# Five SBUF tensors of a matmul stream at other offsets modulo 256 bytes

## What is computed

```python
h  = modulate(rmsnorm(x, norm1_w), shift1, scale1)          # 2048 tokens
hc = modulate(rmsnorm(ctx, norm1_w), ...)                    # 256 context tokens
conf_u, q, k, v, af, ab, r, sc_u = split(h @ w_in)           # one projection, 2848 columns
y = concat([conformer_conv(...), gla_output(...), short_conv(...)]) @ w_out
x = x + gate1 * y
h = modulate(rmsnorm(x, norm2_w), shift2, scale2)
gate, idx = top_k(softmax(h @ router_w).T, 256)              # 16 experts, 256 tokens each
hid = silu(h[idx] @ w1[e]) * (h[idx] @ w3[e])                # per expert, 1024 x 1024 each
x = x + gate2 * scatter_add(gate * (hid @ w2[e]))
out = rmsnorm(x, final_norm_w)
```

## Time and profile before

| | |
|---|---|
| median of 3 runs | 2157.4 us (2153.78 to 2158.72) |
| the profiled execution: time | 2155.37 us |
| its span | 2153.7 us |
| instructions in it | 35092 |
| PE busy | 2074.7 us, 96% |
| PE's share of the chain that ended last | 80% |

### The profile page before, as it was taken

How to read it: one execution, slowest core, us unless ns; L and a number is a source line. 1 busy time by engine, 2 the same in 40 slices (tenths; PEclk the granted TensorE clock), 3 DMA queues, 4 the chain that set the end, 5 groups by cost and what they waited for, 6 DMA issues and landing times.

```text
span 2153.7 us, 35092 instructions
## 1 busy us (share of the span) xinstructions
PE 2074.7 (96%) x13569; PEld 1815.5 (84%) x13569; DVE 1369.9 (64%) x2082; ACT 996.1 (46%) x1631; POOL 277.8 (13%) x357
## 2 busy tenths in 40 slices
PE   6999999999999899997999999999999999999996
PEld 4778888888878677785899999999999999999985
DVE  3664648995994577757555656556555665656557
ACT  5923454444531445431444544445444444445455
POOL 0001000100001010020011122111221112111120
PEclk9999999999999999998999999999999999999998
DMA  7463333333427665456357666576565765657565
GB/s 258 150 248 132 109 106 99 115 118 88 125 77 237 236 208 176 145 214 257 118 204 246 215 215 211 187 264 214 193 216 195 273 198 186 217 218 253 198 233 225
DMA packets 188285, 407.95 MB, mean 189 GB/s; under 512 B 15956, under 2 KB 53396, under 8 KB 187300
## 3 DMA queue, kind: packets, MB, share of 16 engines
q1 hardware_dynamic: 162212, 318.36, 42.6%
q0 software_dynamic: 25984, 88.39, 12.6%
HBM read 329.59 MB, written 77.12 MB: 189 GB/s over the span
## 4 chain that ended last, share of the span: by engine, by line
PE 80%; DVE 10%; ACT 3%; DMA 3%; issue 2%; SPq 1%; POOL 0%; DVEq 0%; ACTq 0%; POOLq 0%
PE bh L55 11%; PE bh L57 11%; PE bh L56 11%; PE bank L55 8%; PE bank L57 8%; PE bank L56 8%; PE eby L55 5%; PE eby L57 5%; PE eby L56 5%; DVE acc L854 3%; PE ebt L2283 1%; PE bank L1031 1%; DVE over L2012 1%; PE bank L1413 1%; DVE raw L2472 1%
## 5 line engine op out<-in xcount | busy, mean ns | idle before, releaser
L55 PE MATMUL bh<-xt_hi,shi 128*128 128x256 f32 x2048 | 572.2, 279 | 3.2 <-DVE slo L2436 2.7
L56 PE MATMUL bh<-xt_lo,shi 128*128 128x256 f32 x2048 | 571.6, 279 | 0.0
L57 PE MATMUL bh<-xt_hi,slo 128*128 128x256 f32 x2048 | 571.4, 279 | 0.0
L2436 DVE TENSOR_TENSOR slo<-raw,shi 128x1024 fp32r<-128x1024 f32 x384 | 456.0, 1221 | 156.9 <-ACT shi L2345 152.4
L2345 ACT ACTIVATE shi<-raw 128x1024 fp32r<-128x1024 f32 x384 | 389.8, 1052 | 127.1 <-PE eby L57 125.5
L55 PEld LDWEIGHTS bh<-xt_hi,shi 128*128 128x128 f32 x2048 | 385.3, 188 | 4.6 <-issue 2.5
L56 PEld LDWEIGHTS bh<-xt_lo,shi 128*128 128x128 f32 x2048 | 385.4, 188 | 0.6
L57 PEld LDWEIGHTS bh<-xt_hi,slo 128*128 128x128 f32 x2048 | 385.3, 188 | 0.0
L55 PE MATMUL bank<-h_hi,whi 128*128 128x512 f32 x704 | 283.4, 403 | 0.0
L57 PE MATMUL bank<-h_hi,wlo 128*128 128x512 f32 x704 | 275.4, 391 | 0.0
L56 PE MATMUL bank<-h_lo,whi 128*128 128x512 f32 x704 | 275.4, 391 | 0.0
(11 more groups left out here) (348 smaller groups left out, 3127.6 us busy)
## 6 DMA issues: line engine op xcount, KB each, us to landing
raw<-in_exp_w_dram SPq DMA_DIRECT2D x96, 2048.0 KB, 11.0
uT<-stage POOLq DMA_DIRECT2D x72, 256.0 KB, 2.7
xb<-in_ada_w_dram SPq DMA_DIRECT2D x24, 512.0 KB, 5.6
wraw<-in_w_in_dram SPq DMA_DIRECT2D x22, 512.0 KB, 5.4
adaw<-in_ada_w_dram SPq DMA_DIRECT2D x8, 1024.0 KB, 9.7
xb<-in_x_dram SPq DMA_DIRECT2D x16, 512.0 KB, 4.2
xt<-in_x_dram POOLq DMA_DIRECT2D x16, 512.0 KB, 5.3
x2d<-xt POOLq DMA_DIRECT2D x16, 512.0 KB, 3.0
```

What stands on the lines that cost most here:

```text
L55: nc.tensor.matmul(out, w_hi, x_hi, start=start, stop=False)
L56: nc.tensor.matmul(out, w_hi, x_lo, start=False, stop=False)
L57: return nc.tensor.matmul(out, w_lo, x_hi, start=False, stop=stop)
L2436: nc.vector.tensor_tensor(item_dst(slo, n), item_src(n), item_dst(shi, n), ALU.subtract).then_inc(S["w_lo_ready"], 1)
```

## The change

No instruction is added, taken away or moved on any engine; one wait is added on ACT. What changes is where tensors stand in SBUF. Modulo 256 bytes:

| product | stationary: before, after | moving: before, after | columns |
|---|---|---|---|
| projection, latents | `whi`, `wlo`: 0, 0 | `h_hi`, `h_lo`: 0, 192 | 512 |
| projection, context | `whi`, `wlo`: 0, 0 | `hc_hi`, `hc_lo`: 0, 192 | 256 |
| output projection | `ct`: 0, 192 | `wo`: 0, 192 | 512 |
| experts, gate and up | `shi[i]`, `slo[i]`: 0, 32 i | `xt`: 32, 192 | 256 |
| experts, down | `ht`: 0, 96 | `shi[i]`, `slo[i]`: 0, 32 i | 512 |

A gap of 192 bytes (`h_gap`) ahead of `h_hi` moves everything behind it, also what is allocated relative to `low` and `high`: the six `raw` buffers, the buffers `xb` and `adaw` that the first loads fill, the states and the tail's tensors all go from 0 to 192. `gap` grows by 64 bytes, so that `whi`, `wlo` and the stages stay at 0. `xs`, into which the tokens of an expert are gathered, goes from 0 to 96. `wraw`, the raw weights of the projection, goes from 224 to 160 (the first tile's too; the third tile's, `wraw2`, from 0 to 192).

To make room, `msq` of `phase_project` lies in `tok`, which is written later, and four small tensors of `phase_experts` become slices of one. `shi[3]` now lies over `found`, which before lay under `slo[2]`; so ACT waits for `list_ready` before it writes item 3 of the first expert. DVE waits for the same semaphore before its first item, before and after.

```diff
-        gap = sb("gap", [P, 8])
+        gap = sb("gap", [P, 24])
...
-        ssq, msq, rst = (sb(n, [P, 18]) for n in ("ssq", "msq", "rst"))
+        ssq, rst = (sb(n, [P, 18]) for n in ("ssq", "rst"))
+        msq = v.tok[:, :, :].rearrange("p e s -> p (e s)")[:, 0:18]
...
+        v.found_free = (S["list_ready"], 1)
...
-        shi = [sb(f"shi{i}", [P, D], F32R) for i in range(NR)]
-        slo = [sb(f"slo{i}", [P, D], F32R) for i in range(NR)]
+
+        def behind(shift):
+            at[0] += (shift - at[0]) % 256
+
+        shi, slo = [], []
+        for i, shift in enumerate((0, 32, 64, 96)):
+            behind(shift)
+            shi.append(sb(f"shi{i}", [P, D], F32R))
+            slo.append(sb(f"slo{i}", [P, D], F32R))
         xs_words = [sb(f"xs{i}", [P, D], F32R) for i in range(2)]
         xs = [t[:, :].bitcast(F32) for t in xs_words]
-        at[0] += 32
+        behind(192)
         xt_hi, xt_lo = sb("xt_hi", [P, KD, CAP], F32R), sb("xt_lo", [P, KD, CAP], F32R)
-        at[0] += 224
+        behind(96)
         ht_hi, ht_lo = sb("ht_hi", [P, FD, CAP], F32R), sb("ht_lo", [P, FD, CAP], F32R)
...
-        ssq, msq, rst, nt = (sb("f_" + n, [P, NT + 2]) for n in ("ssq", "msq", "rst", "nt"))
+        small = sb("f_small", [P, 4 * (NT + 2)])
+        ssq, msq, rst, nt = (small[:, i * (NT + 2):(i + 1) * (NT + 2)] for i in range(4))
...
                 for n in range(NR):
+                    if n == NR - 1:
+                        act.wait_ge(*v.found_free)
                     split(0, n)
...
+                hsb("h_gap", [P, 48])
+                low = nc.sbuf_base
                 v.h_hi, v.h_lo = hsb("h_hi", [P, L // NB, KD, NB], F32R), hsb("h_lo", [P, L // NB, KD, NB], F32R)
```

## The result

The changed kernel takes 2180.4 us (median of 4 runs, 2177.92 to 2181.76) against 2156.1 us (2153.78 to 2158.72) for the kernel before: a ratio of 1.0111, with a 95% interval of 1.0094 to 1.0129. It is slower by 24.3 us, where 11.6 us less had been forecast. The profiled execution took 2177.92 us, with a span of 2176.2.

A forecast was written before the change was run, and what follows sets the result against it. PE's matmul streams were taken as the bound. Savings of 7.0 + 0.8 + 0 + 0 + 3.8 = 11.6 us from the median 2157.4 gave 2146 us, the forecast's own range being 2140 to 2151.

The forecast's parts named there:

- If only equal offsets cost, each saves 3.3 ns: PE's matmul streams: only operands at equal offsets pay extra, 13.2 against 9.9 ns besides columns, so unequal ones save 3.3 ns.
- Latent projection: Projection's 2112 matmuls of 512 columns, distance 0 to 192: each saves 3.3 ns, 7.0 us in all.
- Context projection: Projection's some 150 matmuls of 256 columns, same step: 0.5 us saved, plus 0.3 us for the narrow first tile.
- Output projection: Both operands, ct and wo, go from 0 to 192 and stay equal to each other: nothing.
- Gate and up: Experts' 6144 matmuls, distance 32 to 192, 160, 128 or 96: nothing; bounds 61 us saved, 20 us lost.
- Down product: Experts' 1536 matmuls: three quarters, 1152, become unequal and gain 3.3 ns each, 3.8 us; the fourth buffer stays equal.
- The wait on ACT: ACT's added wait before item 3 of the first expert: nothing, with over 3 us of cover.
- The DMAs: Loads now written off a multiple of 256: nothing taken, upper bound 3 us lost in the first 40 us.
- The rest: Gathered tokens xs, msq in tok and four slices of one tensor, outside PE's streams: nothing.
- the first, that a larger distance would be faster still: Rival: cost falls with distance, so gate and up gain at least 20.3 us more, 2125.5 us; chance 0.2.
- The second, no effect: Rival: offsets do nothing, the 3.3 ns belongs to the stage, time stays at 2157 us; chance 0.2.
- The third, that gate and up lose what they had: Rival: all 6144 gate and up matmuls return to 120.0 ns, 20.3 us lost, 2166 to 2178 us; chance 0.19.

The follow-up runs named there:

- e4_other_half: Kernel before with the split weight buffers at 0, 32, 64, 96, tokens at 64 and hidden values at 224 bytes; 2171.74 us, ratio 1.0077.
- e1_h_back: Changed kernel with the projection, first loads and tail back on a multiple of 256 bytes, experts as changed; 2170.8 us, ratio 1.0068.
- e7_w_beside_h: Changed kernel with the projection's split weights also at 192, beside h, so their distance is 0; 2173.24 us, ratio 1.0078.
- e5_same_distances: Changed kernel with all tensors of the experts' products 64 bytes further on, so every distance stays; 2178.33 us, ratio 1.0103.
- e9_kick_turn: e3_far_gate_up plus one unused float32 transposition on PE ahead of each expert's first item; 2138.09 us, ratio 0.9917 to the kernel before.
- e3_far_gate_up: Kernel before with the tokens xt at 192 bytes in place of 32, all split weight buffers at 0; 2160.03 us, ratio 1.0015.
- e6_far_256_higher: e3_far_gate_up with h and all behind it 256 bytes further on, places modulo 256 kept; 2160.9 us, ratio 1.0024 to the kernel before.
- e10_kick_r: e9_kick_turn with a float32r transposition in place of the float32 one; 2139.9 us, ratio 0.9923 to the kernel before.
- e12_even_128: Kernel before with the tokens xt at 128 bytes, so gate and up have that distance in all buffers; 2173.12 us in one run.
- e13_kick_alone: Kernel before with only a float32 transposition ahead of each expert's gate and up, tokens still at 32; 2161.27 us, ratio 1.0026.

## Why the prediction was wrong

All prices that were measured, in ns for one matmul:

| distance, bytes | 256 columns | 512 columns |
|---|---|---|
| 0 | 119.3 to 120.0 | 226.7 to 228.4 |
| 32 | 116.7 or 117.8 (118.0 in `e4_other_half`) | 233.2 |
| 64 | 117.8 | 229.4 |
| 96 | 119.8 to 120.0 | 233.9 |
| 128 | 118.4 to 118.7, or 119.9 | 233.2 |
| 160 | 120.1 to 120.2 | 233.8 to 234.2 |
| 192 | 113.3 to 114.1, or 117.8; context 116.6 | 232.7 (down), 233.3 (latents) |
| 224 | 118.2 to 118.3 | 232.6 to 233.0 |

**The step that failed** is the reading drawn from the two streams of 256 columns and then used everywhere: "If only equal offsets cost, each saves 3.3 ns". For 512 columns equal offsets are the cheapest, and every other distance costs 2 to 7 ns more. The prediction had two products with 512 columns in its own rows, both at 0, and nothing to compare them with; it took over the price of the other form. It also gave all unequal distances one price, for which it had no reason from a row, since the kernel before had only the distance of 32 in such a stream.

1. *Latent projection*, forecast -7.0 us: the distance of 192 cost 6.5 ns more for each in a steady stretch, and 5.3 over the stage, instead of 3.3 less; 11 us in the stream and 8.3 in the stage. This is the reading's first failure, and `e1_h_back` and `e7_w_beside_h` undo it in two different ways.
2. *Context projection*, -0.5 us: right, from 119.5 to 116.6 ns; the forecast's signal was 116.7. It was the one place where the reading was applied to the form that it was read from, at equal against unequal. The 0.3 us for the narrow first tile had no ground: its slices lie 128 bytes apart, not 512, so that its distances are 0 and 128 by turns, before and after.
3. *Output projection*, nothing: right. Both operands moved to 192 and a matmul took 227.4 ns for 228.1.
4. *Gate and up*, nothing: failed. Unequal distances aren't one price, and one distance isn't either: at 32 bytes the first expert of the kernel before ran at 117.8 ns and the others at 116.7, which the prediction's rows, taken from one expert, did not show. Of the four, 192 gained 2.8 ns in the changed kernel, 128 lost 1.7, 160 and 96 lost 3.0 to 3.4; 8 us in all. The prediction had named this group as the place where it could fail.
5. *Down product*, -3.8 us: failed with the first. Three buffers lost 5 to 7 ns each, 7 us in all, and the fourth kept its 227. The prediction did ask the right question ("if the fourth is no different, it is not equality that costs"): the fourth is different, and it is the cheap one.
6. *The wait on ACT*, nothing: right, the way from the routing to the first expert went from 11.5 to 11.7 us.
7. *The DMAs*, nothing with 3 us as the bound: the bound came true. The first latent matmul is 2.7 us late; it comes at 64.5 to 66.2 us in the five kernels with the loads at 192, and at 62.2 to 63.6 in the eleven others. The mis-sized term rested on `wraw` over the whole span, against `xb`. The program writes `wraw` in pieces of 512 bytes and `xb` in pieces of 4096, so the two differ by more than their offset, and what the offset alone does to a landing can't be read from them; in the first 45 us the rows had the tenth. The rule of the Trainium skill that was weighed there ("DMA: Bandwidth & Descriptors", section "How a descriptor splits into AXI transactions") has the sign right and not the size: the estimate worked out from it gave 19% more beats, and the rate fell by a tenth.
8. *The rest*, nothing: right as far as the stages show.

The rivals: the first, that a larger distance would be faster still, is wrong for this kernel and holds a part of the truth, since 113.4 ns exist at 192. The second, no effect, is refuted by `e1_h_back` and `e7_w_beside_h`. The Trainium skill's page "TensorE: Matmul & The Clock Gate" (section "Step-by-step: what each phase is for") gives the two operands a read port each, and by it the load of the next stationary operand costs the running matmul nothing. The traces do not agree that its place is free: the same 256 columns took 113.9 to 120.2 ns by buffer in the changed kernel and in `e5_same_distances`. Whether the ports are what meets is not shown. The third, that gate and up lose what they had, came about in part: two of the four buffers went to 120 ns and a third to 118.4. It gave 2166 to 2178 us; what it left out is that the projection and the down product lose too.

**What is shown and what is open.** Shown: moving both operands together changes nothing, and moving one changes the price (`e5_same_distances`, `e7_w_beside_h`), in another way for 256 than for 512 columns. That it is the distance modulo 256 rests on less: on the 160 and 416 bytes of the down product, and on the latents and the output projection, whose distances by the program's addresses are 256 and 0 modulo 512 and whose matmuls take 227.9 and 228.1 ns. At one distance a stream can hold to more than one pace for hundreds of matmuls. What precedes it picks one at 192 bytes (the transposition, by `e9_kick_turn` against `e3_far_gate_up`; a stall, one way in `e6_far_256_higher` and the other in `e9_kick_turn`). At 32 bytes both paces stand in the kernel before, and the transposition exchanges them. Open: why. Two readers of the same memory that meet or miss each other would fit, and no run looks at them apart. It is also open why the transposition picks the better pace at 192 and, in fifteen experts, the worse one at 32; why the first expert differs from the rest in the kernel before, `e10_kick_r`, `e12_even_128` and `e13_kick_alone`; and whether the executions without a trace keep the same paces.

**The best version** is `e9_kick_turn`: 0.83% under the kernel before and 1.9% under the changed one. It needs both of its parts, as `e3_far_gate_up` (the distance alone, +0.15%) and `e13_kick_alone` (the transposition alone, +0.26%) show.

## What to carry to other kernels

Before offsets are moved, read what one matmul costs from start to start for each form by itself, and in more than one turn of the loop, since a price read at 256 columns had the wrong sign at 512 and a price read in one expert was not that of another; then change one distance in one stream, and read that stream again. Keep large loads at the start on the offset at which they run now, or price them by the rate in the stretch where nothing hides them. Where a steady stream costs more than it does elsewhere at the same distance, try what stands ahead of it too, and trust only the whole kernel's time.

## What the runs showed of the hardware that was not expected

- With the granted clock at 1.00, the matmuls of one stream take 113.4 to 120.2 ns (256 columns) or 226.7 to 234.3 ns (512 columns) by where their two operands stand to each other modulo 256 bytes and by the pace that the stream has fallen into. The spreads are 6.8 and 7.6 ns.
- A stream keeps its pace: 117.8 ns for 383 matmuls in `e3_far_gate_up`, 113.3 for 359 in `e9_kick_turn`, at the same addresses in the experts' stage. One transposition of 0.1 us ahead of an expert makes the difference, 384 x 4.4 ns = 1.7 us. The kernel before does it by itself: 117.8 ns in its first expert, 116.7 in the others.
- Loads from DRAM into SBUF ran at 385 GB/s into buffers on a multiple of 256 bytes and at 349 GB/s 192 bytes behind one.
